# Expert blocks from two 64-slot units in two column groups, with the output stage's VectorE and ScalarE work reordered by tile

## The reference, cut to what matters

```python
# output of the mixer (gated DeltaNet heads and three dilated attention branches)
ob = sum over 3 branches of outs * softmax(lses)        # per head
ob = rmsnorm(ob, attn_norm)
x = x + gt_a * (concat([oa, ob]) @ w_out)
h = rmsnorm(x, norm_ffn) * (1 + sc_f) + sh_f
# hierarchical mixture of experts: 4 groups of 8 experts
gp = softmax(h @ w_rg);  gprob, gidx = top_k(gp, 1)
el = (h @ w_re).reshape(T, 4, 8)[gidx];  eprob, eidx = top_k(softmax(el), 2)
expert = gidx * 8 + eidx;  gates = gprob * eprob / sum(eprob)
for every expert e and its tokens xb:
    y = (silu(xb @ w_gate[e]) * (xb @ w_up[e])) @ w_down[e]      # 1024 -> 2 x 256 -> 1024
    out[token] += y * gates
x = x + gt_f * out;  return rmsnorm(x, norm_final)
```

## Time and profile before

| | us |
|---|---|
| median of three timed executions | 2570.03 |
| lowest and highest | 2569.0, 2570.17 |
| the profiled execution's own time | 2571.67 |
| its span | 2569.9 |

### The profile page before, as it was taken

How to read it: one execution, slowest core, us unless ns; L and a number is a source line. 1 busy time by engine, 2 the same in 40 slices (tenths; PEclk the granted TensorE clock), 3 DMA queues, 4 the chain that set the end, 5 groups by cost and what they waited for, 6 DMA issues and landing times. The chain is left out here.

```text
span 2569.9 us, 31355 instructions
## 1 busy us (share of the span) xinstructions
PE 2266.6 (88%) x9226; PEld 1341.6 (52%) x9227; DVE 1089.3 (42%) x2271; ACT 785.2 (31%) x2116; POOL 382.9 (15%) x335
## 2 busy tenths in 40 slices
PE   3999899999988896897999978988829999999990
PEld 2666444444444546895777754545524444444440
DVE  5444123323244633556878755666631111111113
ACT  1343111111233301226788753333211111111113
POOL 0000000000111102344332100001021222222220
PEclk9999999999999997998999989989959999999995
DMA  8444113211356527974333233343537977789947
GB/s 345 145 147 131 49 50 106 74 66 58 106 185 201 177 102 240 292 215 156 92 100 106 89 125 128 129 115 125 189 124 239 317 215 233 193 249 316 346 83 284
DMA packets 180608, 426.52 MB, mean 166 GB/s; under 512 B 41432, under 2 KB 81240, under 8 KB 165032
## 3 DMA queue, kind: packets, MB, share of 16 engines
q1 hardware_dynamic: 155944, 346.59, 38.5%
q0 software_dynamic: 15760, 53.65, 9.2%
q10 hardware_dynamic: 8816, 25.18, 3.0%
HBM read 301.04 MB, written 129.04 MB: 167 GB/s over the span
## 5 line engine op out<-in xcount | busy, mean ns | idle before, releaser
L642 PE MATMUL ps<-big,pc_w 128*128 128x512 f32 x1280 | 557.8, 597 | 10.6 <-DMA pc_w<-in_w_chan 10.6
L642 PEld LDWEIGHTS ps<-big,pc_w 128*128 128x128 f32 x1280 | 243.9, 192 | 312.2 <-issue 300.7
L2013 PE MATMUL ps<-big,ex_xt 128*128 x800 | 354.0, 595 | 2.0 <-ACT ex_xt L2053 1.3
L2013 PEld LDWEIGHTS ps<-big,ex_xt 128*128 128x128 f32 x800 | 148.9, 191 | 171.3 <-issue 171.3
L1604 PE MATMUL ps<-w_out,mo_yt 128*128 128x512 f32 x512 | 228.6, 605 | 1.1 <-ACT mo_yt L1828 1.1
L307 PE MATMUL ps<-cp_wt,big 128*128 128x344 f32 x768 | 225.4, 454 | 0.0
L307 PEld LDWEIGHTS ps<-cp_wt,big 128*128 128x128 f32 x768 | 145.9, 191 | 76.9 <-issue 4.1
L2023 PE MATMUL ps<-ex_wd,ex_hidt 128*128 x400 | 180.1, 593 | 3.0 <-DVE ex_y L2075 2.0
L1361 PE MATMUL ps<-at_v,at_pt 128*128 128x128 f32 (+1 forms) x1200 | 182.3, 289 | 0.0
L1427 ACT ACTIVATE at_p<-at_p,at_low 128x256 f32<-128x256 f32 (+1 forms) x384 | 174.0, 456 | 19.2 <-DVE at_low L1390 19.0
L1361 PEld LDWEIGHTS ps<-at_v,at_pt 128*128 128x128 f32 x1200 | 148.7, 191 | 46.1 <-issue 36.4
(11 more groups left out here) (276 smaller groups left out, 2901.0 us busy)
## 6 DMA issues: line engine op xcount, KB each, us to landing
big<-in_w_gate_up SPq DMA_DIRECT2D x32, 2048.0 KB, 11.4
ex_wd<-in_w_down SPq DMA_DIRECT2D x32, 1024.0 KB, 6.6
cp_w<-in_w_ada SPq DMA_DIRECT2D x24, 1024.0 KB, 5.4
ch_d<-pc_cv SPq DMA_DIRECT2D x20, 1024.0 KB, 4.1
at_v<-v_d SPq DMA_DIRECT2D x27, 512.0 KB, 3.9
o_d<-at_o SPq DMA_DIRECT2D x48, 264.0 KB, 2.1
mo<-o_d SPq DMA_DIRECT2D x16, 792.0 KB
pc_qkv<-ch_d SPq DMA_DIRECT2D x16, 768.0 KB, 5.5
```

Source lines behind the costliest of these rows:

```text
L642: last = nc.tensor.matmul(ps[:, n % 2, :], w[:, ch % 2, k, :], m.ht[:, k, g * BANK:(g + 1) * BANK], start=(k == 0), stop=(k == KD - 1))
L2013: last = nc.tensor.matmul(ps[:, 2 + b, :], xt[:, b, k, :], wgu[:, bass.ds(half * WGU + k * 2 * DE, 2 * DE)], start=(k == 0), stop=(k == KD ...
```

## The change

In `experts` a block is two units of 64 slots. An expert has as many units as it needs (at least one), and two units that follow each other make a block, whoever they belong to. The first unit's rows go through columns 0 to 63 of the array into PSUM partitions 0 to 63, with the weights where SyncE put them; the second unit's go through columns 64 to 127 into partitions 64 to 127, with a copy of its expert's weights. ScalarE makes the 128x4096 copy of gate and up weights for block t+2 at the end of its work for block t, VectorE the 128x2048 copy of the down weights for block t+1 at the end of its work. Each copy waits for the announcement of that expert's load. Expert numbers are permuted on the host so that neighbours belong to different groups. Lists are read in halves of 64, with two gathers. SyncE announces expert e-1 before the `y_done` wait of expert e.

In `mix_and_route` the work is cut into smaller functions and dealt to slots of one tile. TensorE takes the halves of y that are there from the start (DeltaNet's) first, and multiplies them before the others are ready. Differences and Exp are made one slot before the weighting. VectorE's slot t is add_out of tile t-1, weigh of tile t+2, place or choose, router_in of tile t-1, normed of tile t+2, differences of tile t+3. SyncE's part of this phase is as before.

```diff
-NBLK = 2 * T // P + NE
+HB = P // 2
+NBLK = (2 * T // HB + NE) // 2
...
-    c[:, C_BLANK:C_END:2] = T + np.arange(P)
+    c[:, C_BLANK:C_END:2] = T + np.arange(P) % HB
...
+        def slots_of(loop):
+            for t in range(5):
+                yield t, t % 2, t // 2
+            with loop(PAIRS - 4) as i:
+                yield i * 2 + 5, 1, i + 2
+                yield i * 2 + 6, 0, i + 3
+            for t in range(13, NT):
+                yield t, t % 2, t // 2
...
+                for n in range(2):
+                    pool.indirect_dma_start(out=lists[:, n * HB:(n + 1) * HB, :].rearrange("p s x -> p (s x)"), out_offset=None, in_=m.list_d.rearrange("r (n s) x -> (r n) (s x)", n=2),
+                                            in_offset=bass.IndirectOffsetOnAxis(ap=coli[:, n:n + 1].bitcast(U32), axis=0)).then_inc(lists_in, 16)
...
# TensorE, mix_and_route
-                turn_y(0, 0)
+                for b in range(2):
+                    turn_half(b, 0, turned)
+                for b in range(2):
+                    pe.wait_ge(*half_taken.n(b + 1))
+                    part(b, range(KD // 2), range(2))
+                    pe.wait_ge(*y_ready[b].n(1))
+                    turn_half(b, 1, yt_done[b])
+                for b in range(2):
+                    if b == 1:
+                        turn_y(0, 1)
+                    pe.wait_ge(*yt_ready[b].n(1))
+                    part(b, range(KD // 2, KD), range(2)).then_inc(*w_done[b].inc)
...
+                part(1, range(KD), range(1)).then_inc(*half_done.inc)
+                logits(1, q - 1)
+                turn_h(0, q)
+                part(1, range(KD), range(1, 2)).then_inc(*w_done[1].inc)
+                logits(0, q)
+                places(q - 1)
+                pe.wait_ge(*ranks_ready.n(q))
+                turn_h(1, q)
+                logits(1, q)
+                places(q)
...
# VectorE, mix_and_route
+                for t, b, q in slots_of(lambda times: link.loop(times, 2 * (PT + RS) + CH + PL)):
+                    if has(t, -1):
+                        add_out(*before(b, q))
+                    if has(t, 2):
+                        weigh(b, q + 1)
+                    if not early(t):
+                        (place if b == 1 else choose)(q - 2)
+                    if has(t, -1):
+                        router_in(*before(b, q))
+                    if has(t, 2):
+                        normed(b, q + 1)
+                    if has(t, 3):
+                        differences(1 - b, q + 1 + b)
...
# SyncE, experts
                         sp.dma_start(wgu[:, b * WGU:(b + 1) * WGU].rearrange("p (k n) -> p k n", k=KD), one(a["w_gate_up"], e)).then_inc(*wgu_in[b].inc)
+                        arrived((b - 1) % NWB, i + (1 if b else 0), i + (2 if b else 1))
                         sp.wait_ge(*y_done.n(free))
                         sp.sem_inc(seen_sp, 1)
                         load_down(e, b)
-                        arrived((b - 1) % NWB, i + (1 if b else 0), i + (2 if b else 1))
...
# TensorE, experts
+                    pe.wait_ge(*wgu2_ready[b].n(q + 1))
                     for k in range(KD):
-                        last = nc.tensor.matmul(ps[:, 2 + b, :], xt[:, b, k, :], wgu[:, bass.ds(half * WGU + k * 2 * DE, 2 * DE)], start=(k == 0), stop=(k == KD - 1))
+                        nc.tensor.matmul(ps[0:HB, 2 + b, :], xt[:, b, k, 0:HB], wgu[:, bass.ds(at * WGU + k * 2 * DE, 2 * DE)], start=(k == 0), stop=(k == KD - 1))
+                        last = nc.tensor.matmul(ps[HB:P, 2 + b, :], xt[:, b, k, HB:P], wgu2[:, b, k, :], start=(k == 0), stop=(k == KD - 1))
...
-                    for n in range(2):
+                    for c in range(2):
                         for k in range(DE // P):
-                            last = nc.tensor.matmul(ps[:, 6 + n, :], hidt[:, b, k, :], wd[:, bass.ds(half * WD + (k * D + n * BANK), BANK)], start=(k == 0), stop=(k == DE // P - 1))
+                            nc.tensor.matmul(ps[0:HB, 6 + c, :], hidt[:, b, k, 0:HB], wd[:, bass.ds(at * WD + (k * D + c * BANK), BANK)], start=(k == 0), stop=(k == DE // P - 1))
+                            last = nc.tensor.matmul(ps[HB:P, 6 + c, :], hidt[:, b, k, HB:P], wd2[:, b, k, c * BANK:(c + 1) * BANK], start=(k == 0), stop=(k == DE // P - 1))
...
# ScalarE, experts
+                def copy_gate_up(t, b):
+                    started = act.value_load(m.by_block[0:1, 0, bass.ds(t, 1)], min_val=1, max_val=NE)
+                    at = act.value_load(m.by_block[0:1, 2, bass.ds(t, 1)], min_val=0, max_val=NWB - 1)
+                    act.wait_ge(*gu_loaded.n(started))
+                    act.sem_inc(seen_act, 1)
+                    nc.scalar.copy(wgu2[:, b, :, :].rearrange("p k n -> p (k n)"), wgu[:, bass.ds(at * WGU, WGU)]).then_inc(*wgu2_ready[b].inc)
...
                     nc.scalar.copy(hidt[:, b, :, :].rearrange("p k n -> p (k n)"), ps[:, 4, 0:DE]).then_inc(*ht_ready[b].inc)
+                    if not tail:
+                        copy_gate_up(t + 2, b)
...
# VectorE, experts
+                def copy_down(t, b):
+                    started = dve.value_load(m.by_block[0:1, 0, bass.ds(t, 1)], min_val=1, max_val=NE)
+                    at = dve.value_load(m.by_block[0:1, 2, bass.ds(t, 1)], min_val=0, max_val=NWB - 1)
+                    dve.wait_ge(*d_loaded.n(started))
+                    dve.sem_inc(seen_dve, 1)
+                    nc.vector.tensor_copy(wd2[:, b, :, :].rearrange("p k n -> p (k n)"), wd[:, bass.ds(at * WD, WD)]).then_inc(*wd2_ready[b].inc)
...
                     if not head:
                         take_y(t - 1, *before(b, q))
+                    if not tail:
+                        copy_down(t + 1, 1 - b)
...
# host
+    def mixed(w):
+        return w.reshape(NG, EG, *w.shape[1:]).swapaxes(0, 1).reshape(w.shape)
```

More of the change, by code:

```diff
@@ L1597, in logits, with part @@
                     last.then_inc(*lg_done[b].inc)
+                def part(b, ks, ns):
+                    for n in ns:
+                        for k in ks:
+                            last = nc.tensor.matmul(ps[:, 2 + 2 * b + n, :], yt[:, b, k, :], w[:, k, n * BANK:(n + 1) * BANK], start=(k == 0), stop=(k == KD - 1))
+                    return last
                 def out(b, q):
@@ L1615, in _ @@
                 for t, b, q in steps(lambda times: pe.Fori(0, times)):
-                    if is_tile(t, 0):
-                        out(b, q)
+                    if first_two(t):
+                        continue
+                    if not is_tile(t, NT - 1):
                         turn_y(*after(b, q))
[L1619 to L1626, removed]
@@ L1627, in _ @@
-                    if not first_two(t):
-                        logits(b, q - 1)
+                    if b == 1 and not early(t):
+                        pe.wait_ge(*ranks_ready.n(q - 1))
+                    turn_h(b, q - 1)
+                    if is_tile(t, NT - 1):
+                        break
+                    out(b, q)
+                    logits(b, q - 1)
                     if b == 0 and not early(t):
                         places(q - 2)
-                for b in range(2):
-                    turn_h(b, PAIRS - 1)
-                    logits(b, PAIRS - 1)
@@ L1747, in _ @@
[L1747 to L1775, removed]
+                differences(0, 0)
+                differences(1, 0)
@@ new lines, in _ @@
+                for b in range(2):
+                    weigh(b, 0)
+                    normed(b, 0)
+                differences(0, 1)
+                for t, b, q in slots_of(lambda times: link.loop(times, 2 * (PT + RS) + CH + PL)):
[11 more added lines that the diff above has]
+                        differences(1 - b, q + 1 + b)
@@ L1781, in _ @@
                 link(V.tensor_copy(pad[:, :], padi[:, :]))
                 link(V.tensor_tensor_scan(ends[:, :], m.ones[:, 0:NE], pad[:, :], 0.0, ALU.mult, ALU.add))
[L1784 to L1787, removed]
-                link(V.tensor_tensor(le[:, :], le[:, :], pad[:, :], ALU.mult))
@@ new lines, in _ @@
+                link(V.tensor_reduce(col[:, 0, :], le[:, :, :], AX.X, ALU.add))
+                for n in range(2):
+                    ins = V.tensor_scalar(eb[:, n, :], m.ones, col[:, 0, n:n + 1], None, ALU.mult)
+                ins.then_inc(*e_ready.inc)
+                link(V.tensor_tensor(le[:, :, :], le[:, :, :], pad[:, :].unsqueeze(1).to_broadcast([P, 2, NE]), ALU.mult))
+                link(V.tensor_reduce(col[:, 1, :], le[:, :, :], AX.X, ALU.add))
+                link(V.tensor_tensor(col[:, 1, :], number[:, :], col[:, 1, :], ALU.subtract))
```

188 lines of the change are left out of this document (124 added, 64 removed).

## The result

The changed kernel takes 2513.5 us, the median of four runs (2507.5 to 2516.3), against 2569.5 for the kernel before: the ratio is 0.978, with a 95% interval of 0.9766 to 0.9795, so 56 us less.

What follows compares the result with a forecast made beforehand. TensorE was taken to bound the experts, VectorE's chain with its waits for ScalarE the output stage. Experts -34.5 and output stage -22.5 sum to -57 from 2570.0, giving 2513; forecast 2514 us, for itself 2490 to 2540, overall 2455 to 2620.

Steps and rivals of the forecast that it cites:

- Number of blocks: Experts: units of 64 give 41 blocks, 42 in pairs, instead of 49, 50 in pairs.
- Slots (26): Experts, gate_up and down: 17 and 9 slots of 0.429 us per block, one lost in each; period 12.55 us.
- Stalls (9 us): Experts: late load announcements delay ScalarE's copy; one 7 us stall near block 14, a few of 1 us; between 0 and 25.
- The copies: Experts: ScalarE's weight copy takes some 3.7 us, VectorE's twice 1.07; ScalarE's costs nothing while the weights are there.
- Start of the output stage: Output stage: half products run under VectorE's first weighting; tile 1's product ends at about 1557 us instead of 1580.
- Loop: Output stage: VectorE waits for a late y load each slot; pair 44.5 us, as before, taking back about 10 us.
- Tail: Output stage, around and after the last product: choose runs under that product and ScalarE's detour goes; -11 us.
- rival 1: Experts: no slot is lost, 24 slots and no price for the change of form; 2468 us, chance 0.12.
- Rival 2: Output stage: loads are not late, a pair takes 36 us instead of 44; 2474 us, chance 0.12.
- Rivals 3 and 4: Experts: column groups overlap partly (slot factor 1.25, 2635 us, chance 0.11) or never (about 2900 us, chance 0.08).
- Rival 5: Experts: weights starve, as loads take longer when blocks are shorter; +30 us, 2544 us, chance 0.10.
- Rival 6: Output stage: gives nothing, since VectorE's chain is only re-dealt; 2536 us, chance 0.08.

Runs made afterwards that it cites:

- aabb: Changed kernel with the column groups' matmuls ordered A A B B in gate_up and down: 2516.5 us, ratio 0.9797 to the kernel before.
- all_a: Changed kernel with all eight gate_up matmuls of column group A, then all eight of B, and A A B B in down: 2717.7 us, one run.
- first_copies: Changed kernel with the weight copies made for the first two blocks only, later copies and their waits removed: 2503.1 us.
- y_first: Changed kernel with SyncE's two output-stage loads of a step exchanged, load of y ahead of load of x: 2451.2 us.
- stage_only: Kernel before with only the output stage's new TensorE, VectorE and ScalarE orders, experts unchanged: 2567.6 us, ratio 0.9992.
- announce_late: Changed kernel with SyncE's expert announcement moved back behind the wait for down and the load of down weights: 2587.3 us.

## Why the prediction held, and where it did not

The total of 2514 us is right to a microsecond, and that is luck: the experts gave 12 us more than forecast and the output stage 12 us less. By the signs that I had set, the forecast of the output stage was wrong: pairs left the 41 to 46 us, the last product ends 0.1 us earlier from attention's end and not 10 to 16, and the experts' phase begins 10.8 us earlier and not 20 to 25.

- *Number of blocks*: right, 42 and 41 periods.
- *Slots (26)*: wrong, it is 24. The step that failed is the reading of the earlier trace rows: I took the third slot of the 64-row group for a slot lost in the order A A B B. `aabb` has that order and loses none. Most of what stood there can be the change of form (two slots of 0.215 and 0.15 for one change are 0.58 of the 0.64 us), though no run tests the groups of rows. I priced the change of form at 0.3 us a block; it is 0.6. The period was 12.0 instead of 12.55, 23 us less over 41 blocks. It is just at the edge of the 12.0 that I had given as a bound. The Trainium skill (TensorE: Matmul & The Clock Gate, Part 3: Packing small matmuls — row/col tiling) gives 2.38 times for three column tiles, and the slot 1.26 times as long for two was my estimate from it. This case doesn't bear the estimate out: two groups ran in the time of one, 0.43 us.
- *Stalls (9 us)*: 18.6, from 510.2 us between the first and the last gate_up's end less 41 x 11.99. (The first of these distances has no down in it and takes 9.4 us, so the stalls themselves are some 21.) The 7 us stall near block 14 came as followed, 6.5 us, but I had not priced the lower clock behind it, 2.1 us. The "few of 1 us" stayed on ScalarE. Nor had I priced TensorE waiting for a gather (6.3) or for nothing visible (4.8); with blocks of 17.2 us, in `all_a`, it waits for neither. Sum for the experts: -46.4 instead of -34.5.
- *The copies*: 3.61 us for 3.7, and 1.23 for 2.1 (I had doubled the 1.07 us of a 128x1024 copy; twice the columns cost 0.16 more). With their waits they cost the 10 us of `first_copies`. That they cost nothing by their work holds only while the weights are there: behind a late announcement the 3.6 us stand in TensorE's path.
- *The moved line*: missing from the prediction. I used the new place when I followed the order by hand and never asked what the old one would give. It carries 74 us, more than the whole gain; without it the change would be slower than the kernel before.
- *Start of the output stage*: right. Tile 1's product ends 24 us earlier, measured from attention's end; I said 23.
- *Loop*: the mechanism is right, L1699 waits for o once a tile in alternating lengths. The size is off: 6.7 and 10.2 us instead of 6.05 and 8.55, since o is there 7.6 and 11.1 us after h (1663.86 - 1656.31; 1688.69 - 1677.64) instead of 7.0 and 9.5. By the ends of the even tiles' products three pairs in a row take 47.5, 47.6 and 47.9 us, beyond my bound of 46, and the fourth 44.4; before it was 44.3. At the last product's end all 24 us of the start are gone: some 21 by the loop, where I had let it take 10, and 3.1 by the two TensorE steps inside the last product. The "-13" was 0. The step that failed is the size of the wait per slot.
- *Tail*: right. From the last product's end to the last TensorE step of the routing are 18.0 us instead of 29.0, -11.0 for -11; but the steps inside the last product, which this term was to cover, lie ahead of that mark. The second gather and what follows cost 0.2 us and not 1.6.
- *Rivals*: rival 1 has the better account of the slots but not of the form. Rival 2 was false for this kernel, and `y_first` shows what it would have been worth: its 2474 was too modest, as I left the pair at 36 and counted only five. Rivals 3 and 4 are excluded by the 24 slots (and the sum of rival 3 at f = 1.25 was off: it gives some 2627 us, not 2635). Rival 5 came with one wait of 6.5 us and no 30. Rival 6, that the output stage gives nothing, is nearest to what `stage_only` measured. No rival was the ring of the announcement.

## What to carry to other kernels

When work is re-dealt so that one wait goes, look up in each queue what stands in front of the transfer that the new order needs first: here two exchanged lines were worth as much as the whole change, and nothing without it. Where an engine is given a wait ahead of time-critical work, follow what that wait needs back to the engine's own next instruction; a ring of 20 us blocks is one line away. A gap of 5 us in TensorE's work cost some 2 us more behind it, at the lower clock. And price a moved line of the diff at both its places, even if it looks like bookkeeping.

## What the runs showed of the hardware

- Two column groups of 64 columns each ran wholly side by side in fp32: starts 10 ns apart, 0.43 us a step, the step of one full-width MATMUL. Changing between them and the full array cost 0.15 us each time.
- A matmul of one group passed one waiting matmul of the other group, but not two: `aabb` cost 0.1 us a block, `all_a` 5.2 us a gate_up.
- Behind waits of 5.3 and 6.5 us TensorE's granted clock was 0.50 (1985 to 1990 us, `announce_late`) and 0.61 (2099.2 to 2105.7 us, the changed kernel), and five steps took 0.85 us instead of 0.43.
- The same 792 KB load was waited for until 6.4 us after its issue (1657.50 to 1663.86) and, in `stage_only`, until 13.4 us after it (1686.21 to 1699.63), in the same stage. From tile to tile short and long waits alternated (the earlier trace rows had shown one value only).
